# Top score level of a chunked linear attention joined with the first step by four, in the gaps of its score slots, with instruction lists in a new order

## What is computed

```python
h = _rmsnorm(x, norm_pre[l])
c = _split_cols(h @ w_in[l])
# A: gated linear attention, 4 heads, decay log_a;  C: HGRN2, 4 heads, decay log_f
o_a, s_gla_new = _chunked_gated_linear(heads(q_a), heads(c['a_k']), heads(c['a_v']), heads(log_a), s_gla)
o_c, s_hgrn_new = _chunked_gated_linear(heads(q_c), heads(k_c), heads(c['c_i']), heads(log_f), s_hgrn)
# B: short gated convolution;  D: trailing means over 2, 4, 8, 16 positions
mix = jnp.concatenate([o_a, o_b, o_c, o_d], axis=-1)
x = x + _rmsnorm(mix @ w_out[l], norm_post[l])
# inside _chunked_gated_linear, per chunk, with b = cumsum(log decay):
decay = jnp.exp(jnp.where(causal, b[t] - b[s], -jnp.inf))
scores = jnp.einsum('bhtd,bhsd,bhtsd->bhts', q, k, decay)
```

## Time and profile before

| | us |
|---|---|
| median of three runs | 1009.53 (1008.88 to 1010.11) |
| the profiled execution's own time | 1009.16 |
| its span, first to last instruction | 1007.3 |
| PE busy | 960.9 (95%) |
| DVE busy | 614.3 (61%) |
| ACT busy | 432.7 (43%) |
| POOL busy | 356.7 (35%) |
| PE's share of the chain that ended last | 78% |

### The profile page before, as it was taken

How to read it: one execution, slowest core, us unless ns; L and a number is a source line. 1 busy time by engine, 2 the same in 40 slices (tenths; PEclk the granted TensorE clock), 3 DMA queues, 4 the chain that set the end, 5 groups by cost and what they waited for, 6 DMA issues and landing times.

```text
span 1007.3 us, 23928 instructions
## 1 busy us (share of the span) xinstructions
PE 960.9 (95%) x10228; PEld 717.7 (71%) x10228; DVE 614.3 (61%) x1069; ACT 432.7 (43%) x845; POOL 356.7 (35%) x456
## 2 busy tenths in 40 slices
PE   2999789999999999999999999999999999999997
PEld 2858567865887668865887668865887668856683
DVE  4897677637745476536744586536844576347654
ACT  6875455522534335423543335432543334324333
POOL 1213442065302660075303660075303660067200
PEclk9997799999999999999999999999999999999999
DMA  8830341001130013101130013001130013001101
GB/s 314 287 110 3 111 153 48 23 1 42 34 95 1 2 64 64 43 1 43 35 93 2 1 64 69 38 2 43 43 85 2 1 64 85 1 2 43 64 5 44
DMA packets 41517, 56.04 MB, mean 56 GB/s; under 512 B 27793, under 2 KB 28603, under 8 KB 41403
## 3 DMA queue, kind: packets, MB, share of 16 engines
q1 hardware_dynamic: 41411, 54.51, 17.2%
HBM read 38.44 MB, written 9.86 MB: 48 GB/s over the span
## 4 chain that ended last, share of the span: by engine, by line
PE 78%; DVE 9%; DMA 5%; ACT 4%; issue 1%; SPq 1%; POOL 1%; DVEq 0%; ACTq 0%; POOLq 0%
PE pj L815 40%; PE op L1065 15%; PE pj L834 7%; DMA xin<-in_x_prompt 2%; DVE xres L1972 2%; PE sc L902 2%; DMA h<-xres 2%; DVE w_lo L1952 2%; PE m L1020 2%; PE m L1045 2%; PE sc L950 1%; PE sc L1085 1%; PE op L1085 1%; PE m L997 1%; PE pj L1037 1%
## 5 line engine op out<-in xcount | busy, mean ns | idle before, releaser
L815 PE MATMUL pj<-h,w_hi 128*128 128x256 f16 (+1 forms) x3456 | 385.1, 265 | 0.1
L815 PEld LDWEIGHTS pj<-h,w_hi 128*128 128x128 f16 x3456 | 310.8, 99 | 48.1 <-issue 5.4
L815 PE MATMUL pj<-h,w_lo 128*128 128x256 f16 (+1 forms) x1728 | 209.0, 264 | 0.0
L815 PEld LDWEIGHTS pj<-h,w_lo 128*128 128x128 f16 x1728 | 158.1, 99 | 17.5
L2075 DVE COPY_PREDICATED A<-cu,sc 64x384 f32<-64x384 uint8 (+1 forms) x168 | 73.9, 440 | 68.0 <-PE sc L902 65.0
L658 POOL TENSOR_TENSOR G<-B 128x256 f32<-128x256 f32 x17 | 12.1, 712 | 185.6 <-DVE B L2005 171.9
L834 PE MATMUL pj<-w_hi,h 128*128 128x512 f16 (+1 forms) x272 | 64.4, 379 | 1.6 <-DVE K L2014 1.2
L1361 ACT ACTIVATE X<-pj 128x512 f32<-128x512 f32 (+1 forms) x45 | 24.9, 553 | 83.5 <-PE pj L815 68.4
L1065 PE MATMUL op<-wo_hi,m_hi 128*128 128x512 f16 x224 | 53.0, 379 | 0.0
L1065 PE MATMUL op<-wo_lo,m_hi 128*128 128x512 f16 x224 | 52.9, 379 | 0.0
L1065 PE MATMUL op<-wo_hi,m_lo 128*128 128x512 f16 x224 | 52.9, 379 | 0.0
(11 more groups left out here) (321 smaller groups left out, 1643.4 us busy)
## 6 DMA issues: line engine op xcount, KB each, us to landing
xin<-in_x_prompt SPq DMA_DIRECT2D x17, 512.0 KB, 4.2
wo_hi<-in_w_units SPq DMA_DIRECT2D x16, 512.0 KB, 5.1
xres<-in_x_prompt SPq DMA_DIRECT2D x15, 512.0 KB, 3.5
out_y_prompt<-xres SPq DMA_DIRECT2D x14, 512.0 KB, 2.6
wo_lo<-in_w_units SPq DMA_DIRECT2D x12, 512.0 KB, 5.5
xres<-in_w_out SPq DMA_DIRECT2D x8, 256.0 KB, 3.4
gpost<-in_w_out SPq DMA_DIRECT2D x8, 256.0 KB, 4.0
m_hi<-in_state_gla SPq DMA_DIRECT2D x1, 512.0 KB, 8.6
```

Source lines behind the costliest of these rows:

```text
L815: m = pe.matmul(b[:, j * T:(j + 1) * T], w[:, k, col + 128 * j:col + 128 * j + 128], h[:, k, :], start=(n == 0 and k == 0), stop=(n == 2 a ...
```

## The change

For tiles from 2 on, level 0 has no step of its own any more. Its matmuls (`top_scores`, 8 of them per branch, same operands) come first in `scores(i, br, 1)` and write into the 32 unused columns of each slot of 128, two slots for one result of 64 columns. `copy_scores(i, br, 1)` makes first the two copies that level 0 made, from the gaps, then its six masked copies. The number of score steps per tile falls from 8 to 6 (`FEWER`, `levels`, `at_score`). GpSimd's exponents of level 2 in branch 0 now wait for the joined step.

The lists are changed too:
- TensorE, loop: out_product(i-1, 0, 0) stands ahead of scores(i, 0, 2), not behind it; attend(i, 1) behind updates(i, 1), not ahead of transpose_keys(i, 1).
- TensorE, tile 8: proj d_z (0) ahead of proj d_v (1) and attend; scores(NT, 1, 2) ahead of both a_z parts; recall(NT, 1) ahead of both b_z parts.
- GpSimd, tile 8: exponents(NT, 1, LAST) ahead of factors(NT, 1, 2).
- ScalarE, tile 8: y_norm(NT-1, 1) ahead of square(NT, 0).
- VectorE, tile 1: pooling(1) ahead of w_out_lower(3); normalise(1, 0) ahead of x_scale(2, 0). Tile 8: gate_abs(NT, "D") ahead of pool_out(NT).

```diff
-FEWER = dict(sc=16, am=16)
+FEWER = dict(sc=12, am=12)
 def levels(i):
-    return (0, 5, 3)[min(i, BY_FOUR)]
+    return (0, 5, 2)[min(i, BY_FOUR)]
 def at_score(i, br, lv):
-    return br * (n + 1) + min(lv, n)
+    return br * (n + 1) + min(lv - 1 if i >= BY_FOUR else lv, n)
...
             elif br == 0:
                 pool.wait_ge(*at("up", i, 0))
-                pool.wait_ge(*at("sc", i, 2 * at_score(i, 0, 0) + 2))
+                pool.wait_ge(*at("sc", i, 2 * at_score(i, 0, 1) + 2))
...
             pe.wait_ge(*at("gm", i, mults_done(i, br, lv)))
+            if i >= BY_FOUR and lv == 1:
+                top_scores(i, br)
...
+        def gaps(t, c):
+            return t.rearrange("p (k t) -> p k t", t=128)[:, 2 * c:2 * c + 2, 96:128]
+        def top_scores(i, br):
+            for c in range(2):
+                for j in range(2):
+                    for hh in range(2):
+                        g = half(g_of(i, br, 0), hh)[:, j, c * CH:c * CH + CH]
+                        pe.matmul(gaps(half(SC[hh], j), c), g[:, 0:64], g[:, 64:CH].rearrange("p (a t) -> p a t", a=2),
+                                  start=True, stop=True)
...
                 values_proj(i, 0, (1,))
-                scores(i, 0, 0)
                 values_proj(i, 1, (0,))
                 values_proj(i, 1, (1,))
                 scores(i, 0, 1)
                 proj(i, "c_q", (0,))
                 proj(i, "c_q", (1,))
+                out_product(i - 1, 0, 0)
                 scores(i, 0, 2)
-                out_product(i - 1, 0, 0)
                 out_product(i - 1, 0, 1)
                 scores(i, 0, LAST)
                 proj(i, "d_v", (0,))
                 proj(i, "d_v", (1,))
-                scores(i, 1, 0)
                 attend(i, 0)
...
-                attend(i, 1)
                 transpose_keys(i, 1)
                 proj(i, "b_v", (0,))
                 proj(i, "b_v", (1,))
                 updates(i, 1)
+                attend(i, 1)
...
-            if lv == (0 if i else LAST) and (i or br):
+            if lv == (LAST, 0, 1)[min(i, BY_FOUR)] and (i or br):
                 dve.wait_ge(*at("va", i, br))
...
+                if lv == 1:
+                    for j in range(2):
+                        m = dve.tensor_copy(A[0:64, j:8:2, 64:CH].rearrange("p k (a t) -> p k a t", a=2),
+                                            half(sc, j).rearrange("p (k a t) -> p k a t", a=2, t=128)[:, :, :, 96:128])
...
-                copy_scores(i, 0, 0)
                 copy_scores(i, 0, 1)
                 copy_scores(i, 0, 2)
                 query_in(i)
...
                 query_decay(i, 0)
-                copy_scores(i, 1, 0)
                 pooling(i)
```

More of the change, by code:

```diff
@@ L786, in _ @@
             exponents(NT, 1, 2)
+            exponents(NT, 1, LAST)
             factors(NT, 1, 2)
-            exponents(NT, 1, LAST)
             factors(NT, 1, LAST)
@@ L1303, in _ @@
             values_proj(NT, 0, (1,))
-            scores(NT, 0, 0)
             out_product(NT - 1, 0, 0)
@@ L1314, in _ @@
             scores(NT, 0, LAST)
+            proj(NT, "d_z", (0,))
             proj(NT, "d_v", (1,))
-            scores(NT, 1, 0)
             attend(NT, 0)
-            proj(NT, "d_z", (0,))
             transpose_keys(NT, 0)
@@ L1326, in _ @@
             recall(NT, 0)
+            scores(NT, 1, 2)
             proj(NT, "a_z", (0,))
-            scores(NT, 1, 2)
             proj(NT, "a_z", (1,))
@@ L1342, in _ @@
             tails_out(NT)
+            recall(NT, 1)
             proj(NT, "b_z", (0,))
             proj(NT, "b_z", (1,))
-            recall(NT, 1)
             proj(NT, "c_z", (0,))
@@ L1916, in _ @@
             gate_in(NT, "D")
+            y_norm(NT - 1, 1)
             square(NT, 0)
-            y_norm(NT - 1, 1)
             gate_log(NT, "D")
@@ L2445, in _ @@
             copy_scores(1, 1, 0)
+            pooling(1)
             w_out_lower(3)
-            pooling(1)
             w_out_lower(4)
@@ L2470, in _ @@
             scale_norm()
+            normalise(1, 0)
             x_scale(2, 0)
@@ L2473, in _ @@
             gate_abs(1, "A")
-            normalise(1, 0)
             y_out(0, 0)
@@ L2549, in _ @@
             forget_sum(NT)
-            copy_scores(NT, 0, 0)
             copy_scores(NT, 0, 1)
@@ L2556, in _ @@
             copy_scores(NT, 0, LAST)
-            copy_scores(NT, 1, 0)
             y_out(NT - 1, 0)
@@ L2563, in _ @@
             y_out(NT - 1, 1)
+            gate_abs(NT, "D")
             pool_out(NT)
-            gate_abs(NT, "D")
             states(NT, 0, 1)
```

## The result

The changed kernel takes **1010.77 us** (median of 21 runs, 1009.82 to 1015.06), the kernel before 1009.12 in the 21 runs beside it: the ratio is 1.0018, 95% interval 1.0009 to 1.0026. It is slower by 0.9 to 2.6 us, the medians differ by 1.65, and the forecast was 3.0 slower. Its profiled execution took 1009.82 us with a span of 1008.0 (before 1009.16 and 1007.3).

The account below looks back on a forecast made before the run. TensorE, busy 111.90 of 112.67 us per steady tile, was taken as the bound, with 0.8 us idle at low_rank. Six tiles +5.0, last tile -2.3, second tile +0.3 sum to +3.0: 1012.5 us (own range 1011.3 to 1014.0).

Parts of the forecast that it names:

- The steady tile: Tiles 2 to 7: +0.84 us each from -0.09 - 0.39 + 0.93 (new wait) + 0.39; six tiles +5.0.
- The joined step: TensorE: top matmuls 0.39 us and by-four step 0.82 both stay; one 0.09 us change saved per tile, in branch 0.
- the moved scores: Branch 1's top scores move behind out_product(i-1, 1, 0), ahead of a_z: +0.39 us per tile in the second stretch.
- The overlap: Steady tile: VectorE's query_silu meets GpSimd's key_product and ends 0.55 us after it, taking about 1.1 us instead of 0.69.
- GpSimd's exponents of level 2 wait: Loop, branch 0: exponents(i, 0, 2) wait for the joined scores, 1.9 us late; a 0.8 stall without the moved out_product.
- The last stretch: Last tile: 0.86 us new GpSimd wait, -2.81 for three removed waits, -0.36 for four changes; sum -2.3 us.
- The three waits of the earlier trace: Last tile, TensorE: waits of 0.41, 1.02 and 1.38 us, all forecast to go.
- The first tile: VectorE's later w_out_lower(3) delays output weights: 0 to +1.2 us, taken as +0.3; normalise(1, 0) gives back at most 0.15.
- The port is no matter: Rival, chance 0.22: query_silu takes 0.69 us beside GpSimd; +0.45 us per tile, +0.7 in all, 1010.2 us.
- The wait doesn't arise: Rival, chance 0.20: out_product(i-1, 1, 0) doesn't wait for yo; -0.09 us per tile, -2.5 in all, 1007.0 us.
- VectorE becomes late for gate_abs(A): Rival, chance 0.10: VectorE's 0.2 us cover is used up; a further 0.5 us per tile, 1015.5 us.
- The last tile doesn't gain: Rival, chance 0.10: in the last tile the new GpSimd wait stays and the old waits re-form; 1014.8 us.

Follow-up runs that it names:

- query_in ahead: Changed kernel with VectorE's query_in(i) ahead of copy_scores(i, 0, 2) in the loop; ratio to the kernel before 0.9967, tile 112.61 us.
- The first experiment: Changed kernel with scores(i, 0, 2) back ahead of out_product(i-1, 0, 0) in TensorE's loop; ratio to the kernel before 1.0034, tile 113.61 us.
- a_z ahead: Kernel before with proj a_z (1) ahead of proj b_c (0) in TensorE's loop; ratio to the kernel before 0.9958, tile 111.88 us.
- the join alone: Changed kernel with every list exchange undone, only the joined score step and its GpSimd wait kept; ratio to the kernel before 1.0039, tile 113.67 us.
- product kept away: Changed kernel with GpSimd's key_product(i, 0) of tiles 2 to 7 also waiting for query_silu; ratio to the kernel before 0.9989, tile 113.06 us.
- old last tile: Changed kernel with tile 8's lists in the order of before; ratio to the kernel before 1.0035, last stretch 144.65 us.
- x_lo ahead: Changed kernel with query_in before copy_scores(i, 0, 2), x_lo(i+1, 0) before gate_abs(A), attend(i, 1) back before transpose_keys(i, 1); ratio to the kernel before 0.9962, tile 112.67 us.
- the kernel with both edits: Changed kernel with query_in ahead of copy_scores(i, 0, 2) and a_z (1) ahead of b_c (0); ratio to the kernel before 0.9942, tile 112.35 us.

## Why the prediction was right

**The whole: +3.0 forecast, +1.65 measured between the medians.** The sign and the mechanism hold; the size was forecast too large. The median of 1010.77 lies just under the forecast's own range (1011.3 to 1014.0), and by the limits that the prediction set itself (slower over 1011.6) it counts as the same, to which it had given 0.27, and 0.48 to slower. The parts below give 4.45 for the six tiles (forecast 5.0), -2.4 for the last stretch (-2.3) and -0.34 for the first tile (+0.3): +1.7 in all. The largest miss, 0.6 us, is the first tile.

**The steady tile: +0.84 forecast, +0.74 measured (4.45 / 6).** Step by step in tile 6, forecast times moved by the 1.63 between the tiles' starts:

| step | forecast | measured |
|---|---|---|
| scores(i, 0, 2) start | 681.33 | 681.13 |
| copy starts | 682.32 | 682.12 |
| query_silu starts | 689.47 | 689.13 |
| query_silu takes | 1.10 | 1.25 |
| y_out ends | 696.21 | 695.93 |
| out_product(., 1, 0) starts | 696.28 | 696.09 |

The mechanism is the one forecast, and the two experiments on it settle it: with the copy moved the wait is gone, with GpSimd held back most of it is gone. Three terms had another size:
- **The joined step is shorter than its parts.** The sum kept 0.39 and 0.82 us. The chain shows

```profile
669.62 0.39 PE sc L941 x16
670.01 0.66 PE sc L904 x32
```

  which is 1.05, not 1.21. So a step of its own between projections costs 0.25 more than its matmuls in company (these 0.16 and the 0.09 of the change), where the prediction had taken the 0.09 alone. In branch 0 this is a gain ahead of the copy (the 0.20 of the first two rows), in branch 1 it makes the price of the moved scores 0.23 instead of 0.39. The gaps of the slots cost nothing: the top scores still take 0.39.
- **The overlap was sized right, by its end.** The prediction let query_silu end 0.55 after GpSimd's instruction, as in the last tile; it ended 0.54 after it (690.38, 689.84). It takes 1.25 and not 1.10 only because it began earlier in GpSimd's instruction than forecast. So what counts is where GpSimd's instruction ends, not when query_silu begins. The Trainium skill, SBUF — State Buffer, section "Who interferes with whom", calls the ports that the two engines share an exclusive lock, and says of VectorE's two-port modes that whoever issues first has them for the whole instruction. Read so for this instruction too, the end would be 0.69 behind, and the runs show 0.14 to 0.15 less, as far as the spans of GpSimd can be trusted.
- **A stop not foreseen, at head_sums of branch 0.** VectorE's states(i, 0, 1) stands behind the branch's copies and y_out(i-1, 1) in its list and runs 1.1 us later against TensorE's out_product(i-1, 1, 0) than before, 0.24 for the top scores ahead of it on TensorE and 0.86 for the two copies; its cover was some 0.7. VectorE, and then the chain of tile 6:

```profile
715.78 0.47 DVE L2147 SCALAR_TENSOR_TENSOR S<-S,dec,m 128x64 f32<-128x64 f32 x2
```

```profile
713.65 2.73 PE pj L815 x24
716.40 1.10 PE m L1059 x4
```

  states ends at 716.25, and with the 0.14 that a release takes elsewhere in this chain that is 716.39; head_sums starts at 716.40. It hardly waits, but its four matmuls take 1.10 us on the chain, where they took 0.86 before, as other matmuls do here behind a stop. That adds 0.24 ahead of a_z. The prediction saw VectorE's lateness, but followed it to gate_abs(A) only. No run tried states alone, but it shows directly in tile 4, where y_out(i-1, 1) idles 0.46 us within itself, in the kernel before as well, and states comes later still:

```profile
489.45 1.10 PE L1059 MATMUL m<-X,cf 128*128 128x256 f32 x4 [0.37 <-DVE S L2147]
```

  There gate_in(A) comes 0.35 us later in its tile than in the others; in the kernel before that difference was 0.01. The stop belongs to the join and not to the late y_out: in tile 6 head_sums takes these 1.10 us, 0.14 or 0.15 behind the end of states, also with query_in ahead and with TensorE's old order.

Before a_z, then, +0.23 and +0.24 stand where +0.39 was forecast. The errors nearly cancel within the tile (tile 6, +0.85 in all: +0.26 up to out_product(i-1, 1, 0) where the forecast had +0.45, +0.49 from there to a_z, +0.10 in the x chain); that the sum was met to 0.1 is partly luck.

**Covers.** gate_abs(A) started 0.49 us after VectorE was free; the forecast was 0.2, so it held:

```profile
727.26 0.69 DVE L2293 SCALAR_TENSOR_TENSOR X<-X 128x512 f32<-128x512 f32 x1 [0.49 <-ACT X L1371]
```

GpSimd's exponents of level 2 wait 1.92 us (forecast 1.9) with no one late for it, thanks to the moved out_product. The first experiment showed what that cover is worth: 0.92 us (forecast 0.8).

**The last stretch: -2.3 forecast, -2.4 measured.** The rows that decide it:

```profile
906.42 0.81 PE L904 MATMUL sc<-G 64*64 64x96 f32 x28 [0.95 <-POOL G L600]
...
928.82 0.46 PE L941 MATMUL sc<-h 64*64 64x64 f32 x16 [0.37 <-POOL G L600]
```

The first is the 0.86 of the forecast. The second is a further wait that it had not; the shorter joined steps (0.16 each, two in the tile) about pay for it. The three waits of the earlier trace rows are gone, and y_out(NT-1, 1) starts 2.4 us sooner in its tile, as forecast (78.55 us behind the tile's start and not 80.95).

**The first tile: +0.3 forecast, -0.34 measured.** Between attend(1, 0) and out_product(0, 0, 0) the changed kernel is 0.36 us slower (27.64 for 27.28 on the chain), and from there to tile 2 it is 0.34 faster. The prediction's delay of the output weights would show in the first part, but the other kernels' traces say that it isn't there. What goes with the 0.36 is the mean granted clock from 125 to 150 us, 1.00 before and 0.93 after (the third number from the end):

```profile
125.00:150.00 25.00, 21.18 (x277) 17.67 (x275) 18.65 (x38) 13.37 (x25) 10.87 (x14) 1.00 0.46 149
```

```profile
125.00:150.00 25.00, 22.25 (x269) 17.93 (x268) 18.64 (x38) 13.39 (x24) 11.14 (x14) 0.93 0.44 140
```

Ten traces, five at each of these clocks (start of attend to start of out_product, and from there to log_alpha(2), the last step ahead of tile 2's first c_f, in us):

| VectorE's list in tile 1 | clock | to out_product | from there on |
|---|---|---|---|
| old: before, a_z ahead | 1.00 | 27.21, 27.22 | 33.98, 33.96 |
| old: the join alone | 0.93 | 27.58 | 33.97 |
| new: query_in ahead, product kept away, both | 1.00 | 27.20, 27.21, 27.22 | 33.63, 33.63, 33.63 |
| new: changed, scores first, old last tile, x_lo ahead | 0.93 | 27.57, 27.59, 27.58, 27.64 | 33.64, 33.63, 33.63, 33.63 |

The first part follows the clock and not the list: with the same clock the two lists are the same to 0.1 us, so the way over the DMAs had cover, and the forecast's term of 0 to +1.2 was nothing. The second part follows the list and not the clock: the new one saves 0.34. In the kernel before, and also in the one with the join alone, the chain here runs through gate_abs(1, A), normalise(1, 0) and y_out(0, 0), and TensorE stops for it; before:

```profile
166.32 1.06 PE op L882 x8
```

In the changed kernel the chain doesn't leave TensorE here, and these eight take 0.87 us. So it is normalise(1, 0), moved ahead, that wins 0.34 where the prediction gave it at most 0.15; that it is this exchange and not the one of w_out_lower is read from the chain, no run has them apart. That the first row of the result's table came out at 0.0 is chance: the changed kernel's profiled execution had the lower clock there.

**Against the rivals.** "The port is no matter" fell with the row of 1.25 us, and with the 0.69 that query_silu takes when GpSimd is held back. "The wait doesn't arise" fell in the changed kernel, but the kernel with query_in ahead is that rival made true: -0.14 us per tile where it said -0.09. "VectorE becomes late for gate_abs(A)" fell here, and came true in the kernel with both edits. "The last tile doesn't gain" fell.

## What to carry to other kernels

Joining two steps saves little on the bound engine (some 0.25 us here) and makes two things later: whoever reads the joined result, and whoever may reuse its buffers. Follow both to where they next meet the bound engine, at every place where they do (here out_product, scores and head_sums), before judging. Where a step of the bound engine is moved later, move with it what stands behind its reader in the reader's list: one line of VectorE's list was worth 0.9 us per tile here (113.51 to 112.61), while the join, with both of its waits removed, leaves 0.14. And when a wait is to be removed, ask for every link into it; of two chains of nearly equal length, shortening one gives nothing.

## What the runs showed of the hardware

**The granted clock of one and the same code differs between executions, and moves the rest of the run.** Kernel before, from 50 to 113 us (us, then busy PE, PEld, DVE, ACT, POOL, granted clock, DMA share, GB/s):

```profile
50.00:113.00 63.00, 53.86 (x884) 38.59 (x881) 51.14 (x125) 40.93 (x112) 20.34 (x30) 0.84 0.14 47
```

The kernel with query_in ahead, whose lists are the same there:

```profile
50.00:113.00 63.00, 54.63 (x848) 40.35 (x847) 50.32 (x123) 38.09 (x103) 19.40 (x29) 0.79 0.13 46
```

At a mean granted clock of 0.79 it did 36 matmuls fewer in the same time, and it reached tile 2 at 193.89 instead of 190.78. Over all ten traces attend(1, 0) starts between 120.01 (granted clock 0.85 from 50 to 113 us, 0.94 from there to 125) and 125.82 us (0.79 and 0.67). That is more than all that this change does, and why a profiled span (1007.3 for both of these) says less than its tiles. Starts of tiles are the measure to compare two traces by, and the times need many runs: 31 of the kernel before lay between 1007.2 and 1013.3 us, 24 of them up to 1010.8 and the other seven, all with a mean clock of 0.982, from 1012.5 on.

**VectorE and GpSimd hold each other in turn.** A VectorE instruction that takes 0.69 us alone, begun while GpSimd's product was under way, ended 0.54 to 0.55 us behind that product's end in three cases: query_silu in the last tile and in tile 6 (above), and gate_abs(A) with x_lo ahead. In the last of these the hold also runs the other way first. x_lo, begun 1.0 us ahead of GpSimd's product, takes its 1.28 us; the product takes 1.40 and not 1.27; and gate_abs(A), begun 0.39 into the product, takes 1.56 and not 0.69:

```profile
725.96 1.40 POOL L706 TENSOR_TENSOR K<-K,G 128x512 f32<-128x512 f32 x1 [13.35 <-ACT G L1547]
```

```profile
724.95 1.28 DVE L1982 SCALAR_TENSOR_TENSOR xres<-xin,sx,xres 128x1024 f16<-128x1024 f32 x1
726.35 1.56 DVE L2293 SCALAR_TENSOR_TENSOR X<-X 128x512 f32<-128x512 f32 x1
```

In the changed kernel x_lo began 0.05 us behind the start of the product, took 2.31 us and ended 1.09 behind the product's end.
